# A transformer-like two-block kernel on one core: the last add of the attention output moves from GpSimd to VectorE

## The reference, cut to what matters

```python
DILATED_PATTERNS = ((128, 1), (512, 4), (2048, 16))

def second_block(x, ...):
    h = rmsnorm_2(x, g_norm[layer])
    a_u, a_v, a_gate, q, k, v, b_gate, gate_logits = jnp.split(h @ w_in[layer], splits, axis=-1)
    y_a = chunked_spatial_gating(...) * jax.nn.silu(a_gate)
    y_b = dilated_attention(q, k, v) * jax.nn.silu(b_gate)
    g_a, g_b = jnp.split(jax.nn.sigmoid(gate_logits), N_BRANCHES, axis=-1)
    merged = g_a * (y_a @ w_proj_a[layer]) + g_b * (y_b @ w_proj_b[layer])
    x = x + merged @ w_out[layer]
    return rmsnorm_2(x, g_final)
```

## Time and profile before

| what | value |
|---|---|
| median of 3 runs | 2304.27 us (2302.86 to 2304.69) |
| the profiled execution's own time | 2305.84 us |
| its span | 2304.1 us |
| PE busy | 2286.8 us (99%) |
| DVE busy | 1248.2 us (54%) |
| ACT busy | 936.0 us (41%) |
| POOL busy | 842.7 us (37%) |
| mean granted TensorE clock | 0.997 |

### The profile page before, as it was taken

How to read it: one execution, slowest core, us unless ns; L and a number is a source line. 1 busy time by engine, 2 the same in 40 slices (tenths; PEclk the granted TensorE clock), 3 DMA queues, 4 the chain that set the end, 5 groups by cost and what they waited for, 6 DMA issues and landing times.

```text
span 2304.1 us, 30731 instructions
## 1 busy us (share of the span) xinstructions
PE 2286.8 (99%) x11062; PEld 1912.3 (83%) x11062; DVE 1248.2 (54%) x1831; ACT 936.0 (41%) x1476; POOL 842.7 (37%) x565
## 2 busy tenths in 40 slices
PE   9999999999999999999999999999999999999999
PEld 7888888888888888888888888888888888878887
DVE  6444773864444442236855444567677777642435
ACT  5422232333333331124244222467777777631112
POOL 4322222355555543322365455522233222323322
PEclk9999999999999999999999999999999999999999
DMA  4111222232222243322321322433443434353223
GB/s 169 65 47 37 92 85 98 73 155 83 83 83 83 83 164 102 100 74 110 128 87 55 115 99 94 164 111 98 123 119 109 126 103 128 97 187 128 104 106 119
DMA packets 93971, 241.00 MB, mean 105 GB/s; under 512 B 30928, under 2 KB 35504, under 8 KB 93744
## 3 DMA queue, kind: packets, MB, share of 16 engines
q1 hardware_dynamic: 77504, 183.50, 24.4%
q10 hardware_dynamic: 16368, 56.15, 6.1%
HBM read 179.18 MB, written 60.42 MB: 104 GB/s over the span
## 4 chain that ended last, share of the span: by engine, by line
PE 97%; DVE 2%; DMA 1%; issue 0%; ACT 0%; SPq 0%; DVEq 0%; ACTq 0%
PE dense L942 19%; PE dense L943 19%; PE dense L944 19%; PE dense L1134 10%; PE dense L1135 10%; PE dense L1136 10%; PE aux L1283 1%; PE aux L1282 1%; PE aux L1337 1%; PE aux L1312 1%; PE aux L1330 1%; PE aux L1309 1%; PE aux L1223 1%; PE aux L1305 1%; PE aux L1088 1%; PE aux L1326 0%
## 5 line engine op out<-in xcount | busy, mean ns | idle before, releaser
L801 POOL TENSOR_TENSOR w_lo<-w_raw,w_hi 128x512 fp32r<-128x512 f32 x246 | 381.6, 1572 | 1052.3 <-ACT w_hi L1448 1043.2
L942 PE MATMUL dense<-x_hi,w_hi 128*128 128x512 f32 x1424 | 567.1, 398 | 1.9 <-DVE x_lo L2108 1.8
L943 PE MATMUL dense<-x_lo,w_hi 128*128 128x512 f32 x1424 | 557.8, 392 | 0.0
L944 PE MATMUL dense<-x_hi,w_lo 128*128 128x512 f32 x1424 | 557.4, 391 | 0.0
L1448 ACT CAST w_hi<-w_raw 128x1024 fp32r<-128x1024 f32 x121 | 127.3, 1052 | 538.7 <-PE dense L944 524.1
L944 PEld LDWEIGHTS dense<-x_hi,w_lo 128*128 128x128 f32 x1424 | 268.2, 188 | 58.2
L857 POOL TENSOR_TENSOR w_lo<-w_sums,w_hi 128x512 fp32r<-128x512 f32 x144 | 230.1, 1607 | 228.9 <-ACT w_hi L1614 228.8
L942 PEld LDWEIGHTS dense<-x_hi,w_hi 128*128 128x128 f32 x1424 | 268.7, 189 | 49.5 <-DVE x_lo L2108 2.2
L943 PEld LDWEIGHTS dense<-x_lo,w_hi 128*128 128x128 f32 x1424 | 269.0, 189 | 44.9
L1134 PE MATMUL dense<-x_hi,w_hi 128*128 128x512 f32 x576 | 225.7, 392 | 1.1 <-DVE work L2440 0.9
L1135 PE MATMUL dense<-x_lo,w_hi 128*128 128x512 f32 x576 | 224.2, 389 | 0.0
(11 more groups left out here) (332 smaller groups left out, 3839.6 us busy)
## 6 DMA issues: line engine op xcount, KB each, us to landing
w_raw<-weights SPq DMA_DIRECT2D x163, 512.0 KB, 3.6
w_raw_b<-weights SPq DMA_DIRECT2D x34, 512.0 KB, 4.2
kept_qkv<-work ACTq DMA_DIRECT2D x24, 512.0 KB, 3.2
kept_m<-work ACTq DMA_DIRECT2D x22, 512.0 KB, 2.6
work<-kept_m SPq DMA_DIRECT2D x22, 512.0 KB, 3.3
residual<-xT SPq DMA_DIRECT2D x16, 512.0 KB, 6.9
kept_x<-residual ACTq DMA_DIRECT2D x16, 512.0 KB, 2.6
att_q<-kept_qkv SPq DMA_DIRECT2D x32, 256.0 KB, 4.7
```

The costliest lines, as they stand in the source:

```text
L801: last = pool.tensor_tensor(WL[:, u.slot, at4], WR[:, u.slot, at4], WH[:, u.slot, at4].bitcast(f32), ALU.subtract)
L942: pe.matmul(dst, WH[:, u.slot, k], hi, start=(k == 0), stop=False)
L943: pe.matmul(dst, WH[:, u.slot, k], lo, start=False, stop=False)
L944: last = pe.matmul(dst, WL[:, u.slot, k], hi, start=False, stop=(k == nk - 1))
```

## The change

`sum_y` goes from GpSimd's program into VectorE's `o_out`, directly behind the add into `OT` on which it waits. The operands, the access patterns and the semaphore `yb_up` stay as they are. It is done 16 times: in every odd stage that has a `done` (15 of them: eight stages 3 and seven stages 1), and once behind the stages. GpSimd's wait on `w_lo` ahead of each `sum_y` goes too.

```diff
@@ GpSimd @@
             def stage(pair, m, before=None, done=None, head=True):
                 if before:
                     split(pair.unit(m).plus(1))
-                if m % 2 and done:
-                    pool.wait_ge(w_lo, pair.unit(m).plus(1).count(1))
-                    sum_y(*done)
                 if m == 1 and done:
                     gate_y(done[0])
...
-            def sum_y(pair, m):
-
-                h = m // 2
-                pool.wait_ge(yh, pair.count(4, m + 1))
-                hi, lo = (OT[0:DH].rearrange("p (r e a) -> p e r a", r=4, e=2)[:, e] for e in range(2))
-                pool.tensor_tensor(by_class(Y[h * DH:(h + 1) * DH, HALF:S]), hi, lo, ALU.add).then_inc(yb_up, 1)
...
             split(Unit(U_PA + 1))
-            pool.wait_ge(w_lo, U_PA + 2)
-            sum_y(Pair(PAIRS - 1), 3)
             gate_y(Pair(PAIRS - 1))
@@ VectorE, o_out @@
                 if sb:
                     rest = OT[0:DH].rearrange("p (x c) -> p x c", x=2)
                     dve.tensor_tensor(rest, late_o(slice(0, DH)), rest, ALU.add).then_inc(yh, 1)
+                    dve.wait_ge(yh, pair.count(4, m + 1))
+                    hi, lo = (OT[0:DH].rearrange("p (r e a) -> p e r a", r=4, e=2)[:, e] for e in range(2))
+                    dve.tensor_tensor(by_class(Y[h * DH:(h + 1) * DH, HALF:S]), hi, lo, ALU.add).then_inc(yb_up, 1)
```

## The result

The changed kernel takes 2315.39 us (2314.98 to 2318.19, 6 runs) against 2303.82 us (2301.60 to 2304.69, 6 runs) of the kernel before: 11.6 us more by the medians. The direction was forecast and so was the place; the size, 6.2 us, was about half of it, and the time lies above the stated range.

The account below looks back on a forecast made before the run. TensorE, fully busy over the stages, was taken to bound the kernel. Its waits, 7 x 0.57 + 8 x 0.27 = 6.2 us, on the median 2304.27 gave 2310.5 us; whole range 2303.8 to 2314.

Parts of the forecast that it names:

- What bounds the kernel: Over the stages TensorE is busy 487.00 of 487.00 us, so only waits of TensorE count.
- The add alone: Between `O` and `r5` in odd stages: the add takes 0.68 us, using up the margin before `s7`, at no cost.
- The stride of the result: The add writes every fourth column: no cost taken; bounds at most 0.9 us in 15 stages, far end +9.2 us.
- the third rival: Add dearer by its stride, or `s0` and cast late: +0.2 to +0.6 us per odd stage, 2313.5 to 2319.5; chance 0.11.
- The add beside GpSimd: In odd stages GpSimd's second weight split holds the add, which ends 0.55 us behind the split's end.
- What PE then waits: At `s7`, which waits for `r5`: TensorE loses 0.57 us in a stage 1, 0.27 us in a stage 3.
- Whether it is given back: Over the stages TensorE has no idle time, so nothing absorbs the loss and the next stage finds the same offsets.
- The 16-byte line: Each element of the add's result crosses to a new SBUF line; penalty put at a few hundredths of a us.
- What goes from GpSimd, and the 16th add: GpSimd's next products start up to 1.3 us earlier, worth 0; the add behind the stages, 0.68 us, costs 0.
- The first one: At `s7`: the split doesn't hold the add, the margin just holds, 0 us lost, 2304.3; chance 0.15.
- The second: Behind the stages: the 1.2 GHz stretch gets shorter, -3.4 us, in sum +2.8, 2307.1; chance 0.12.
- The fourth: Behind the stages: lighter GpSimd ends a TensorE wait and half the slow stretch, 6.5 us faster, 2297.8; chance 0.02.

Follow-up runs that it names:

- tail: Kernel before, GpSimd's weight split behind the stages held until VectorE scaled the third group of late probabilities: 2301.62 us against 2303.44, ratio 0.9994.
- micro: Kernel before with single VectorE adds and copies behind its end, GpSimd idle; only durations read: add 0.68 us contiguous, 1.05 us at 16 bytes.
- swap: Changed kernel with the two heads' results of the moved add exchanged between the partition halves of y: 2317.58 us (2 runs).

## Why the prediction was wrong, point by point

- *What bounds the kernel.* Right. The loss stood as a wait of TensorE at `s7`, in every kernel that was slower.
- *The add alone, 0.68 us.* Wrong, and this is the step that failed, in its part "The stride of the result", where no cost was taken. It is 1.05 to 1.07 us alone and 0.91 instead of 0.55 us behind the split's end. That is 0.37 us in each of 15 stages, 5.5 us, and nearly the whole gap between 6.2 and 11.6 or 12.1. The yardstick was the fault: L2518, a strided copy, was compared with a contiguous add, when a contiguous copy takes 0.69 us, as L2117 in the trace of the kernel before could have told. The far bound, 1.29 us of GpSimd, was named and given 0.11 with the third rival, 2313.5 to 2319.5, in which the time now lies; the range was cut at 2314.
- *The add beside GpSimd.* Right. All 15 adds end 0.91 to 0.95 us behind the split; with the splits moved away, 7.0 us of the 11.6 go. The rule of the Trainium skill that was weighed there ("SBUF — State Buffer", section "Who interferes with whom") agrees with these 15 adds.
- *What PE then waits.* Right in kind: 0.57 + 0.37 and 0.27 + 0.37 give 0.94 and 0.64, and 1.06 and 0.59 were measured. The rest is where `r5` starts. The prediction had it 0.08 us ahead of the add's end in both; it is 0.04 us behind it in stages 1 (+0.12) and 0.14 us ahead in stages 3 (-0.06).
- *Whether it is given back.* Right in the main: 11.2 of 11.55 us stay over the 14 stages of the table.
- *The 16-byte line.* The Trainium skill's penalty for a new line ("SBUF — State Buffer", section "Door 1: The DMA port swizzle") was said to be borne out for a few hundredths only. The single adds bear it out: nothing at 8 bytes, where two elements fall into a line, and 0.37 us in 512 columns at 16 bytes, where one does. The same note of the Trainium skill also says that one can stride 4 fp32 for free. Read as a step of four elements, which is this add's, that does not hold: 1.05 us against 0.68.
- *What goes from GpSimd, and the 16th add.* Right, 0 both: with the add later on VectorE the time is that of before. The 16th is 1.07 us, not 0.68, and as free: from the last `O` to the end of the span it is 264.88 us before and 264.89 after.
- *The rivals.* The first one came out as soon as both its conditions were made true, 2303.92 us. The second, a shorter stretch at 1.2 GHz behind the stages, did come in the profiled execution, 3.4 us instead of 9.9, and with the missing early one makes the profiled pair 9.3 us apart and not 11.6. But in runs of the kernel before alone the mean granted clock goes from 0.997 to 1.000, so the length of these stretches varies without the change, and the medians differ by what the stages lost. It moved single executions. The third is what happened, by its first condition, the stride. The fourth did not come; its wait is the one that `tail` takes away by moving the split, which the change leaves where it was.

## What to carry to other kernels

An instruction that moves to another engine keeps its operands' patterns but not its price: take its duration there from a row of the same operation with the same stride, and judge a strided row only by a contiguous one of its own kind. Where a queue feeds the bound engine just in time, look for the place at which that queue itself waits for the bound engine; the same add cost 11.6 us in front of `r5` (4.6 with no split beside it) and nothing behind `r6`. Before an add of two SBUF tiles goes to VectorE, look at what GpSimd does in that microsecond.

## What the runs showed of the hardware that was not expected

- VectorE, 512 float32 columns: an add takes 0.68 us with a result contiguous or 8 bytes apart, 1.05 us at 16, 1.07 us at 32 bytes, 1.03 us at 512 bytes, and 1.13 us with both inputs read 1 KB apart. A copy of 1024 columns goes from 0.69 to 1.14 us with a result written 1 KB apart. GpSimd took 1.29 us for the 16-byte add, as it did for an L801 that is contiguous and twice as tall.
- An instruction that doesn't wait for the one ahead starts 0.07 to 0.15 us ahead of its end, but 0.02 to 0.04 us behind it when that one wrote the upper half of the partitions and the next writes from the first one on (`micro`, changed kernel, `swap`).
- A scaling of 128x256 with one tile as input takes 0.34 us, and 1.4 us beside a weight split on GpSimd (`tail`); `r5`, also with one input in SBUF besides PSUM, takes 0.40 us beside one.
